# Last expert of a mixture layer: order of its token tiles, PSUM banks and closing vector work; list tables built in three parts

## The reference

```python
x = layer_norm(ALPHA * x + mix, ln_mix_g, ln_mix_b)
# router: the best of 4 groups by its top-2 sum, then the top 2 experts in it
hdn = silu(xb @ w_gate[e]) * (xb @ w_up[e])      # w_gate, w_up: 1024 x 512
y   = hdn @ w_down[e]                            # w_down: 512 x 1024
ffn = sum over a token's two experts of gate * y
x = layer_norm(ALPHA * x + ffn, ln_moe_g, ln_moe_b)
```

## Time and profile before

| what | value |
|---|---|
| median of 3 runs | 1730.23 us (1728.27 to 1732.82) |
| profiled execution: its time, its span | 1730.61 us, 1729.1 us |
| mean granted TensorE clock | 0.974 |
| busy PE, weight load, DVE, ACT, POOL | 94%, 82%, 63%, 38%, 21% of the span |
| chain that ended last, by engine | PE 37%, DVE 3%, issue 2% |
| experts stage | about 994 us to the end |

### The profile page before, as it was taken

How to read it: one execution, slowest core, us unless ns; L and a number is a source line. 1 busy time by engine, 2 the same in 40 slices (tenths; PEclk the granted TensorE clock), 3 DMA queues, 4 the chain that set the end, 5 groups by cost and what they waited for, 6 DMA issues and landing times. The chain is left out here.

```text
span 1729.1 us, 25291 instructions
## 1 busy us (share of the span) xinstructions
PE 1626.9 (94%) x9514; PEld 1416.2 (82%) x9514; DVE 1082.3 (63%) x1672; ACT 659.0 (38%) x917; POOL 358.5 (21%) x277
## 2 busy tenths in 40 slices
PE   8999999999999999999996469999999999999993
PEld 6888888888888888888885468999999999999982
DVE  5446866368673586835765756555676667666676
ACT  3234323244331532414433224344455455444450
POOL 0100125000160000710004012222333333232332
PEclk9999999999999999999998769999999999999997
DMA  6322535323352224442236726676777777777761
GB/s 206 124 73 74 183 108 199 98 74 129 126 210 97 79 93 172 163 145 82 98 122 210 278 80 191 191 211 212 226 238 240 225 240 251 253 227 242 249 186 57
DMA packets 121229, 287.90 MB, mean 167 GB/s; under 512 B 14945, under 2 KB 17121, under 8 KB 120593
## 3 DMA queue, kind: packets, MB, share of 16 engines
q1 hardware_dynamic: 93840, 197.07, 33.6%
q0 software_dynamic: 26688, 87.05, 16.9%
q10 hardware_dynamic: 576, 2.10, 0.3%
HBM read 241.19 MB, written 48.40 MB: 167 GB/s over the span
## 5 line engine op out<-in xcount | busy, mean ns | idle before, releaser
L499 DVE TENSOR_TENSOR mix_w_low<-mix_w_raw,mix_w_high 128x2048 fp32r<-128x2048 f32 x73 | 167.3, 2291 | 164.1 <-ACT mix_w_high L368 164.0
L747 PE MATMUL mix_acc<-mix_xT_high,mix_w_high 128*128 128x512 f32 x640 | 254.0, 397 | 0.6 <-DVE mix_w_low L499 0.3
L749 PE MATMUL mix_acc<-mix_xT_high,mix_w_low 128*128 128x512 f32 x640 | 249.9, 391 | 0.0
L748 PE MATMUL mix_acc<-mix_xT_low,mix_w_high 128*128 128x512 f32 x640 | 249.1, 389 | 0.0
L368 ACT ACTIVATE mix_w_high<-mix_w_raw 128x2048 fp32r<-128x2048 f32 x73 | 139.7, 1914 | 253.8 <-PE mix_acc L749 244.8
L1675 DVE TENSOR_TENSOR moe_gate_up_low<-kept_w_gate_up_raw,moe_gate_up_high 128x2048 fp32r<-128x2048 f32 x64 | 146.6, 2290 | 81.0 <-ACT moe_gate_up_high L1547 81.0
L2002 PE MATMUL moe_gate_psum<-moe_xT_high,moe_gate_up_high 128*128 128x288 f32 x512 | 154.2, 301 | 1.4 <-DVE moe_xT_low L1692 1.4
L2004 PE MATMUL moe_up_psum<-moe_xT_high,moe_gate_up_low 128*128 128x288 f32 x512 | 152.1, 297 | 0.0
L2003 PE MATMUL moe_up_psum<-moe_xT_low,moe_gate_up_high 128*128 128x288 f32 x512 | 151.8, 296 | 0.0
L2003 PE MATMUL moe_gate_psum<-moe_xT_low,moe_gate_up_high 128*128 128x288 f32 x512 | 151.7, 296 | 0.0
L2002 PE MATMUL moe_up_psum<-moe_xT_high,moe_gate_up_high 128*128 128x288 f32 x512 | 151.5, 296 | 0.0
(11 more groups left out here) (387 smaller groups left out, 3577.5 us busy)
## 6 DMA issues: line engine op xcount, KB each, us to landing
mix_w_raw<-in_w_in SPq DMA_DIRECT2D x57, 1024.0 KB, 5.3
kept_w_gate_up_raw<-in_w_gate SPq DMA_DIRECT2D x32, 1024.0 KB
kept_w_gate_up_raw<-in_w_up SPq DMA_DIRECT2D x32, 1024.0 KB
kept_w_down_raw<-in_w_down SPq DMA_DIRECT2D x32, 1024.0 KB, 10.2
mix_w_raw<-in_w_out SPq DMA_DIRECT2D x16, 1024.0 KB, 5.1
mix_x_rows<-in_x POOLq DMA_DIRECT2D x16, 512.0 KB, 4.3
kept_conv_or_residual<-in_x POOLq DMA_DIRECT2D x16, 512.0 KB, 5.0
x<-kept_conv_or_residual POOLq DMA_DIRECT2D x16, 512.0 KB, 3.7
```

What stands on the lines that cost most here:

```text
L499: dve.tensor_tensor(wl[:, stage % 2], raw[:, stage % 2], wh[:, stage % 2].bitcast(F32), ALU.subtract).then_inc(split_l, 1)
L747: pe.matmul(out, ah, bh, start=first, stop=False)
L748: pe.matmul(out, ah, bl, start=False, stop=False)
L749: return pe.matmul(out, al, bh, start=False, stop=last)
```

## The change

Nothing is computed that was not before; one float32 result is made of the same parts.

1. The list tables (`list_one_hots`) come in three parts, one each after `h_low(r, e, 2)` in experts 0, 1 and 2, and the product and `lists` that use them move from expert 1 to expert 3, with PE's wait for `lists_done`, which now stands ahead of expert 4's rows.
2. In the last expert DVE norms the first of expert 14's two row tiles ahead of `hidden(r, LAST, 0)`, and the second one at the old place, ahead of the last hidden tile.
3. On PE the last expert does A, then U, then B. B goes as two halves of 12 matmuls (`down_end`) into the banks `pg[0]` and `pu[0]`, with the tiny matmul between them. Its wait for A's sums is gone; the first half waits for hidden tile 2, and signals by `end_half`.
4. On DVE the order is: row statistics, A's sums, U's sums, B's first half, quarters, B's second half, the norms of U, B and A, and the row tiles' norms last. Each half now has its sum and its statistics one after the other (`end_add`).
5. ACT makes the reciprocal deviations in the order A, U, B. POOL does the three writes back first, as soon as all statistics are there, then stores U, B, A, and the last list's three row tiles at the end.

```diff
+            def end_add(r, k, q):
+                width = DQ if k == U else BANK
+                part = END_IN[k][:, q * BANK:q * BANK + width]
+                from_ps = px[1][:, 0:DQ] if k == U else (py, end_ps)[k][q][:]
+                ...
+                own.step(dve.scalar_tensor_tensor(out=part, in0=from_ps, scalar=scale, in1=part,
+                                                  op0=ALU.mult, op1=ALU.add))
+                wait_apart(dve, idle, *own.due(r))
+                own.step(dve.bn_stats(end_stats[:, k, q], part))
...
                     split_gu(r, n + 1)
+                    if e == LAST:
+                        row_norm(r, LAST - 1, 0, 1)
                     hidden(r, e, 0)
...
-                    if e == 1:
+                    if e == 3:
                         lists(r)
                     hidden(r, e, 2)
                     h_low(r, e, 2)
-                    if e == 0:
-                        list_one_hots(r)
-                    row_norm(r, e - 1)
+                    if e < 3:
+                        list_one_hots(r, e)
+                    row_norm(r, e - 1, 1 if e == LAST else 0)
...
                 row_stats(r, LAST)
+                end_sums(r, A)
                 end_sums(r, U)
+                dve.wait_ge(end_half, r + 1)
+                dve.wait_ge(end_in[B], r * 16 + 16)
+                end_add(r, B, 0)
                 end_quarters(r)
-                end_norm(r, 0, U)
-                end_sums(r, A)
+                end_sums(r, B)
+                end_norm(r, 1, U)
+                end_norm(r, 2, B)
+                end_norm(r, 0, A)
                 row_norm(r, LAST)
-                end_norm(r, 1, A)
-                end_sums(r, B)
-                end_norm(r, 2, B)
...
                     else:
+                        down(r, e, A)
                         down_last(r, e)
-                        down(r, e, A)
+                        pe.wait_ge(hid_done, r * (NE * FC) + NE * FC - 1)
+                        down_end(r, 0)
                         pe.wait_ge(end_sq_done, r + 1)
                         pe.matmul(px[0][:, 0:2], same[:], end_sq[:], start=True, stop=True).then_inc(end_mean, 1)
-                        down(r, e, B)
+                        down_end(r, 1)
```

More of the change, by code:

```diff
@@ L1660, in _ @@
                 row_rstd(r, LAST)
-                for n, k in enumerate((U, A, B)):
+                for n, k in enumerate((A, U, B)):
                     end_rstd_of(r, n, k)
@@ L1879, in row_stats, with row_norm @@
                 ins.then_inc(var_done, 1)
-            def row_norm(r, e):
+            def row_norm(r, e, first=0, end=RTILES):
                 if e not in BATCH:
@@ L1886, in row_norm @@
                 dve.wait_ge(rs_done, r * len(BATCHES) + BATCHES.index(e) + 1)
-                for n, i in enumerate(BATCH[e]):
+                for n, i in list(enumerate(BATCH[e]))[first:end]:
                     rows = R[row_tile(i)]
@@ L2013, in turn_x @@
                     pe.wait_ge(same_done, r + 1)
-                if k == A and e == 2:
+                if k == A and e == 4:
                     pe.wait_ge(lists_done, r + 1)
@@ L2037, in gate_up, with down_end @@
                 ins.then_inc(gu_used, 1)
+            def down_end(r, q):
+                s = slice(q * BANK, (q + 1) * BANK)
+                for c in range(FC):
+                    ins = three(end_ps[q][:], hTh[:, c, AT[B]], hTl[:, c, AT[B]], dh[:, c, s], dl[:, c, s],
+                                c == 0, c == FC - 1)
+                ins.then_inc((end_half, b_used)[q], 1)
             def down(r, e, k):
                 if k == B:
-                    if e < LAST:
-                        for done in (y_act, y_dve):
-                            pe.wait_ge(done, r * (2 * LAST) + 2 * e + 1)
-                    else:
-                        pe.wait_ge(end_sum, r * COLS + 2)
+                    for done in (y_act, y_dve):
+                        pe.wait_ge(done, r * (2 * LAST) + 2 * e + 1)
                 elif e:
```

113 lines of the change are left out of this document (57 added, 56 removed).

## The result

The changed kernel takes **1720.34 us** (median of 4, 1718.38 to 1721.99) against 1730.10 us (median of 4, 1728.27 to 1732.82) of the kernel before: ratio 0.9942, 95% interval 0.9930 to 0.9954, so 8 to 12 us less. Its profiled execution took 1720.39 us, with a span of 1718.9 us and a mean granted clock of 0.975 (before 1729.1 and 0.974).

The account below looks back on a forecast made before the run. PE's matmuls bound the experts, DVE's list and then POOL's the end. 8.2 us at the end plus 1.5 us in the first expert, 9.7 us off the 1730.23 us median, gave 1720.6 us; range 1717.0 to 1725.5.

Parts of the forecast that it names:

- tables, gain: First expert: list tables in three parts fit where DVE is idle and remove PE's gap, 1.5 us gained, bounds 0 and 1.7.
- The rival that another wait takes the gain: Experts: the next wait absorbs the gain from the list tables, giving 1722.1 us; chance 0.04.
- DVE no longer waits for the hidden tile (2.0): Last expert: one row tile moved ahead lets DVE start the last hidden tile without that wait, 2.0 us.
- the 4.5 us: Kernel end: DVE's last norm done at 1713.5 instead of 1718.05, 4.5 us earlier.
- The writes back are covered: POOL at the end: eight issues finish at 1712.7, 1.7 us before the last one at 1714.4, so they are covered.
- the exclusion: Skill's SBUF rule: two-input DVE instructions block POOL's SBUF reads throughout; by it some 3 us gained in place of 9.7.
- the slower case: POOL at the end: issues at the scatter's price, 3.77 us each, make the kernel slower, 1737 us; chance 0.03.
- The rival charged a whole norm: POOL at the end: each issue waits out a 1.28 us norm, 2.56 us per issue, 1727.4 us; chance 0.05.
- POOL issues of 1.7 us and more: Sign of being wrong, at the end; above 1.69 us per issue POOL becomes the bound.
- The forecast of +0.2 us: After POOL's last issue: the fixed 6.3 us grow by 0.2, since a store beside vector work took 1.17, not 0.97.
- The clock rival: Last expert: clock falls in PE's new 1.2 us gap, B's second half takes 5.2 not 2.8 us, 1723.0 us; chance 0.08.
- Rows late: Last expert: a store served between the last gathers delays row statistics by up to 1.3 us, 1721.9 us; chance 0.10.

Follow-up runs that it names:

- experiment 12: The changed kernel again with no edit, as a control: 1721.34 us, ratio 0.9956 against the kernel before.
- experiment 2: The kernel before with only the list tables in three parts, product and wait moved with them: ratio 0.9991 against the kernel before.
- experiment 1: The changed kernel with the list tables, their product and PE's wait as before: ratio 0.9955 against the kernel before.
- experiment 5: The changed kernel with both row tiles of expert 14's batch ahead of the last hidden tile, as before: ratio 0.9964 against the kernel before.
- experiment 6: The changed kernel with U's product ahead of A's on PE: ratio 0.9967 against the kernel before.
- experiment 3: The changed kernel with the three writes back at the end of POOL's list: ratio 0.9968 against the kernel before.
- experiment 10: experiment 7 plus the last list's first row tile normed by ACT and POOL instead of DVE: ratio 0.9950 against the kernel before.
- experiment 7: The changed kernel with one last-list row tile normed between quarters and B's second half, and stored first: ratio 0.9938 against the kernel before.
- experiment 8: The changed kernel with the last three row tiles normed and stored in reverse order: ratio 0.9949 against the kernel before.
- experiment 9: experiment 7 plus the list product on PE in two halves in expert 3: ratio 0.9946 against the kernel before.
- experiment 4: The kernel before with only the three writes back moved ahead of B's store: ratio 0.9996 against the kernel before.
- experiment 11: experiment 9 and experiment 10 together: ratio 0.9943 against the kernel before.

## Why the prediction was right

The forecast of 1720.6 us lies 0.3 us from the median. That it is so close is luck: the same kernel had a median of 1721.34 us in experiment 12. But its parts held too, to some tenths each. By its own steps, in the order of the prediction:

| step | forecast | measured |
|---|---|---|
| tables, gain | 1.5 | 1.7 in the traces, 1.6 in experiment 2 |
| last sigmoid to row statistics | 2.4 | 1683.45 - 1681.18 = 2.27 |
| row statistics | 4.1 | 1687.53 - 1683.45 = 4.08 |
| A's sums and statistics | 3.4 | 1690.87 - 1687.53 = 3.34 |
| U's | 1.6 | 1692.48 - 1690.87 = 1.61 |
| PE idle before the tiny matmul | 1.2 | 1.10 |
| DVE waits for B's second half | 1.2 | 1.37 |
| B's second half and aggregate | 1.85 | 1697.88 - 1695.93 = 1.95 |
| three row tiles | 7.5 | 1711.52 - 1703.83 = 7.69 |
| last issue behind DVE's end | 0.9 | 0.88 |
| a POOL issue ahead of it | 1.17 | 0.98 to 1.00 for six, 1.17 for two; in experiment 12 one of 2.05 |

**The tables.** The step that the parts fit where DVE is idle is shown by the 1.77 and 0.77 us of idle time left, and by experiment 1, where the gap comes back. The rival that another wait takes the gain is refuted by experiment 2.

**The end on DVE.** "DVE no longer waits for the hidden tile (2.0)" is confirmed by experiment 5, without the clock's share. That A's product runs while the hidden tile is made is experiment 6. No experiment takes away by itself that B's halves go into banks of their own, or that all statistics stand ahead of the norms. What these are worth is only read from the traces: the waits of 0.67 and 0.60 us for ACT's deviations are gone. What the prediction didn't see is that part of the 4.5 us was a matter of the clock: of the 2.85 us that DVE waited for the quarters before, 1.4 were PE at the 1.2 GHz level, and experiment 2 did without them. The changed kernel doesn't have that gap and lost nothing to the clock there in either of its traces (the profile after, experiment 12); the kernel before loses it in some executions. With a trace of before like that of experiment 2, the same working would have given 1.4 us less gain.

**POOL.** The writes back are covered (experiment 3: 3.85 us if they aren't). Here the forecast was right and its argument was not. It held against the exclusion that the stores at this place, 1.17 us, "show no such wait". They do, a short one: the store at 1705.17 began 0.32 us before the end of the norm instruction that DVE was running (from 1704.21, 1.28 us long), and was done 0.85 us after that.

This shows once each issue is laid beside what DVE runs when it begins. In the changed kernel, a quarter scatter that began within a subtraction with two inputs from SBUF, and one that began with DVE idle; then the long store of experiment 12:

```profile
1657.83 2.29 DVE L1679 TENSOR_TENSOR moe_gate_up_low<-kept_w_gate_up_raw,moe_gate_up_high 128x2048 fp32r<-128x2048 f32 x1 [2.42 <-ACT moe_gate_up_high L1551]
1658.09 3.46 POOL L1456 DMA_INDIRECT gathered<-moe_y_quarter_rows,moe_scatter_quarter_row  x1 [0.30 <-issue]
...
1615.57 1.56 POOL L1456 DMA_INDIRECT gathered<-moe_y_quarter_rows,moe_scatter_quarter_row  x1 [0.30 <-issue]
```
```profile
1704.16 1.28 DVE L1897 SCALAR_TENSOR_TENSOR kept_w_gate_up_raw<-kept_w_gate_up_raw,moe_row_mean_var,kept_conv_or_residual 128x1024 f32<-128x1024 f32 x1
1704.24 2.05 POOL L1490 DMA_INDIRECT out_x<-kept_w_gate_up_raw,moe_scatter_row  x1 [0.30 <-issue]
```

The first waits 2.03 us for the subtraction's end and takes 1.43 behind it; the last waits 1.20 and takes 0.85. That is the scatter's 3.47 us, on which the slower case rested: it was held by an instruction of 2.29 us, and norm instructions are 1.28.

So the exclusion is true of issues as well, but an issue waits only for the rest of the instruction that runs when it begins; one that begins just ahead of an instruction isn't held. The rival charged a whole norm, 1.28 us, to every issue, and that was its error. A held issue ends 0.85 us behind the norm instruction, and the next begins 0.30 later, when at most 0.2 us of the next instruction are left: 1.02 us, the issue behind the one of 2.05. From then on POOL goes at DVE's pace. By these rows I estimate that a full wait costs about 1.1 us once and not eight times, and 1.19 us were to spare. The six issues of 0.98 us began within 0.1 us of a norm instruction's start, so it is by luck that none was held in that trace.

The prediction's sign of being wrong, "POOL issues of 1.7 us and more", was met by one issue in experiment 12, and nothing was lost: what counts is their mean. The same section of the Trainium skill (SBUF — State Buffer, Who interferes with whom) adds, as an inference, that such a DVE instruction takes only the shared read interface, while making descriptors needs the write interface. By that an issue would not be held, and these rows speak against it.

**The tail.** The forecast of +0.2 us met the number (+0.19), but not by its reason: it had the last issue at 1.17 us, and it took 0.97. Tails without rows lie between 6.30 and 6.52 us in all traces, so 0.2 is scatter. What does move the tail is whether the last store carries rows, 1.2 us, and the prediction did not have that term. It would have been wrong by that much with three full tiles.

**The clock rival** did not come, at a gap of 1.10 us, and its mechanism is real: experiments 5, 6 and 10 show it at 2.36 to 3.38 us, with 1.5 us on DVE's path in the first two. The prediction had priced it at 2.4, with B's second half at 5.2 us in place of 2.8.

**Rows late** did not come in either trace of the changed kernel; in experiments 3, 7, 8 and 9 it did, with 0.18 to 0.33 us. The forecast had the rows land at the same moment as DVE's own low part, and that is how close it is.

## What to carry to other kernels

At the end of a kernel, list for each engine what is still to be done when the last dependent result arrives, and move there only what covers something else: here the independent row tiles on DVE covered eight of POOL's nine issues, and the same issues moved without that cover (experiment 4) gained nothing that could be measured. An idle time of PE can cost more than its length: here gaps up to 1.57 us left the clock alone, and behind nine of the ten from 2.36 us on it fell. In four traces that put 1.4 to 1.7 us on DVE's path, in the others little or nothing. So a late step that widens such a gap can be charged twice. An issue of POOL beside vector work should be priced by what is left of the instruction on DVE when it begins. And cut two traces at events that both have, since 10 us of 1730 don't show in any share of the page.

## What the runs showed of the hardware

- **The granted clock after PE's idle times.** It stayed at 1.00 behind gaps of 1.10 to 1.57 us in every trace (13 gaps in the experts), and fell to 0.50 behind those of 2.36, 2.51, 3.38 and 3.39 us and three of 3.68 and 3.69. Behind 3.56 us it fell before, as behind experiment 4's 3.55, and stayed in experiment 2 (DVE's wait for the quarters: 2.85, 3.09 and 1.43 us). So the length of a gap doesn't decide alone. What else does is open.
- **It fell without any idle time** behind 32 matmuls of 18 columns, in two of twelve traces with the same instructions, for 1.5 us. PE counts as busy all through.
- **DVE and POOL.** An instruction of DVE on 128 single values took 2.16 and 2.17 us in place of 0.21 beside an elementwise instruction of POOL (experiments 10 and 11). In all fourteen traces from 1040 us on, POOL's issues of indirect DMAs took 0.88 to 1.01 us (gathers, stores, writes back) or 1.56 to 1.64 us (scatters) if DVE ran no elementwise instruction with two inputs from SBUF when they began (1044 issues, 269 of them beside other DVE instructions). The 770 that began within such an instruction took what was left of it plus 0.73 to 0.98 us (quarter scatters: plus 1.42 to 1.46). Within 0.1 us of a norm instruction's start it went either way: 0.97 to 0.99 us, in five traces with a norm instruction at 1.33 in place of 1.28, or 2.05 us (experiments 6, 9 and 12).
- **The last store.** 1.2 us less from issue to the end of the span if all its rows are out of bounds.
